# Up projections in split precision: one product over high and low activations, summed afterwards by VectorE

## The reference

```python
def sq_relu_mlp(h, w1, w2):                    # h 256 x 1024, w1 1024 x 4096, w2 4096 x 1024
    return jnp.square(jax.nn.relu(h @ w1)) @ w2
...
    u = rms_norm(x, ln2) @ w_up                # first block, the same with its residual
    return x + jnp.square(jax.nn.relu(u)) @ w_down
```

## Time and profile before

| | |
|---|---|
| median of 3 runs | 1900.62 us (1900.02 to 1901.37) |
| profiled execution, its own time | 1899.04 us |
| its span, first to last instruction | 1897.2 us |
| TensorE busy | 1821.4 us (96%), 11210 products |
| TensorE weight loads (overlap the products) | 1563.8 us, 11210 |
| VectorE busy | 1104.4 us (58%) |
| ScalarE busy | 916.0 us (48%) |
| mean granted TensorE clock | 0.984 of full speed |
| loads | 342.49 MB, mean 181 GB/s |

### The profile page before, as it was taken

The page is one execution under the profiler, slowest core; times in us unless marked ns, Lnnn a source line. Parts: engine busy times, 40 slices in busy tenths (PEclk is TensorE's granted clock), DMA queues, the critical chain, the costliest instruction groups (busy, mean ns, idle before and its releaser), DMA issues.

```text
span 1897.2 us, 26341 instructions
## 1 busy us (share of the span) xinstructions
PE 1821.4 (96%) x11210; PEld 1563.8 (82%) x11210; DVE 1104.4 (58%) x1247; ACT 916.0 (48%) x1211; POOL 38.4 (2%) x32
## 2 busy tenths in 40 slices
PE   7899999998999999999999999999999999989998
PEld 6768999787789989777899997778999787768997
DVE  4866555476665555466655555676555655766554
ACT  5455444354444445454545544645444545545442
POOL 0000000000000000000000000000000000000000
PEclk9999999899999999999999999999999999999999
DMA  7464656653656657653665555536665656344662
GB/s 243 134 214 145 197 180 196 202 167 130 214 178 185 192 189 233 207 193 129 211 194 183 189 184 184 193 111 200 188 189 188 213 176 216 109 163 149 185 190 77
DMA packets 228237, 342.49 MB, mean 181 GB/s; under 512 B 9909, under 2 KB 118809, under 8 KB 227993
## 3 DMA queue, kind: packets, MB, share of 16 engines
q1 hardware_dynamic: 226928, 339.45, 55.4%
q10 hardware_dynamic: 1192, 1.36, 0.2%
HBM read 339.74 MB, written 1.05 MB: 180 GB/s over the span
## 4 chain that ended last, share of the span: by engine, by line
PE 90%; DVE 5%; ACT 2%; issue 2%; POOL 1%; ACTq 0%; DVEq 0%; POOLq 0%
PE PS L1763 14%; PE PS L1765 14%; PE PS L1764 14%; PE PS L1805 9%; PE PS L1806 9%; PE PS L1807 9%; DVE LO L1114 1%; PE PS L2179 1%; PE PS L2149 1%; PE PS L2202 1%; PE PS L2131 1%; PE PS L2190 1%; PE PS L1838 1%; PE PS L2151 1%; PE PS L2150 1%
## 5 line engine op out<-in xcount | busy, mean ns | idle before, releaser
L1114 DVE TENSOR_TENSOR LO<-RAW,HI 128x2048 fp32r<-128x2048 f32 (+1 forms) x274 | 621.5, 2276 | 431.7 <-ACT HI L619 430.9
L619 ACT CAST HI<-RAW 128x2048 fp32r<-128x2048 f32 (+1 forms) x274 | 515.9, 1891 | 265.9 <-PE PS L1765 226.7
L1805 PE MATMUL PS<-AH,HI 128*128 128x256 f32 x1424 | 407.5, 286 | 2.2 <-DVE AL L1561 1.8
L1806 PE MATMUL PS<-AL,HI 128*128 128x256 f32 x1424 | 405.5, 285 | 0.0
L1807 PE MATMUL PS<-AH,LO 128*128 128x256 f32 x1424 | 405.3, 285 | 0.0
L1805 PEld LDWEIGHTS PS<-AH,HI 128*128 128x128 f32 x1424 | 276.3, 194 | 5.8 <-issue 5.2
L1806 PEld LDWEIGHTS PS<-AL,HI 128*128 128x128 f32 x1424 | 276.1, 194 | 1.1 <-issue 0.5
L1807 PEld LDWEIGHTS PS<-AH,LO 128*128 128x128 f32 x1424 | 275.9, 194 | 0.0
L1763 PE MATMUL PS<-HI,AH 128*128 128x512 f32 (+2 forms) x704 | 257.6, 366 | 0.0
L1765 PE MATMUL PS<-HI,AL 128*128 128x512 f32 (+2 forms) x704 | 252.0, 358 | 0.0
L1764 PE MATMUL PS<-LO,AH 128*128 128x512 f32 (+2 forms) x704 | 251.7, 358 | 0.0
(11 more groups left out here) (269 smaller groups left out, 1880.7 us busy)
## 6 DMA issues: line engine op xcount, KB each, us to landing
RAW<-in_w_ff SPq DMA_DIRECT2D x96, 1024.0 KB, 5.4
RAW<-in_w_in SPq DMA_DIRECT2D x80, 1024.0 KB, 5.2
RAW<-in_w_mod SPq DMA_DIRECT2D x48, 1024.0 KB, 5.1
RAW<-in_w_up SPq DMA_DIRECT2D x32, 1024.0 KB, 5.4
RAW<-in_w_down SPq DMA_DIRECT2D x32, 1024.0 KB, 5.0
RAW<-in_w_o SPq DMA_DIRECT2D x12, 1024.0 KB, 5.0
RAW<-in_w_out SPq DMA_DIRECT2D x8, 1024.0 KB, 6.2
RAW<-in_w_attn_out SPq DMA_DIRECT2D x6, 1024.0 KB, 5.7
```

Of the source, the lines that this page charges most:

```text
L619: return nc.scalar.copy(dst, src)
L1114: tt(LO[:, c % RAW_N, 0:n], RAW[:, c % RAW_N, 0:n], HI[:, NTH[c] % HL_N, 0:n].bitcast(F32), ALU.subtract).then_inc(s_lo, 1)
L1805: mm(o, wh, ah[:, j, :], start=j == 0, stop=False)
L1806: mm(o, wh, al[:, j, :], start=False, stop=False)
```

## The change

AH and AL become the two parts of one tile AHL, so that one moving operand of 2 × 256 columns holds both (two runs, 8 KB apart in each partition). For 14 of the 16 up chunks of each MLP (`wide`: all but j = 0 and 1 of i = 0), `features_wide` issues for each q and inner block one product wH·[aH | aL] of 512 columns into a whole bank, and one product wL·aH of 256 columns into that bank's first half. q = 0 and q = 1 have a bank each: 4 and 5 for odd j, 6 and 7 for even j. The result is the sum of a bank's two halves. ScalarE copies the first halves of both banks into U2 (`s_up`), VectorE adds the second halves (and frees the banks), and relu, square and remainder then read U2. The copy and the addition stand ahead of `ahead` in the code. TensorE has one wait more ahead of the transposes of i = 3, since their banks 6 and 7 are now also those of up chunks.

```diff
-        AH = sb("AH", [P, KT, S], F32R)
-        AL = sb("AL", [P, KT, S], F32R)
+        AHL = sb("AHL", [P, 2, KT, S], F32R)
+        AH, AL = AHL[:, 0, :, :], AHL[:, 1, :, :]
...
+        def wide(i, j):
+            return i > 0 or j > 1
+        def copies(q, i, j):
+            return 14 * q + 4 * i + j - 1
+        def wide_banks(j):
+            return 4 if j % 2 else 6
...
 # ScalarE, mlp
                     for j in range(8):
+                        if j < 4 and wide(i, j):
+                            b = wide_banks(j)
+                            act.wait_ge(s_used, c + 8 * i + j + late.n + 1 + HL_N)
+                            act.wait_ge(s_hl, 16 * q + 4 * i + j - 1)
+                            cast(U2[:, j % 2, :].rearrange("p (a n) -> p a n", a=2),
+                                 PS[:, b:b + 2, 0:256]).then_inc(s_up, 1)
                         ahead(c + 8 * i + j + late.n)
...
-                            act.wait_ge(s_used, c + 8 * i + j + late.n + 1 + HL_N)
-                            nc.scalar.activation(RL[:, j % 2, :], PS[:, 4 + (u + j) % 2, :], ACT.Relu).then_inc(s_rl, 1)
+                            if wide(i, j):
+                                act.wait_ge(s_ufree, u + 4 * i + j + 1 + 2)
+                                up = U2[:, j % 2, :]
+                            else:
+                                act.wait_ge(s_used, c + 8 * i + j + late.n + 1 + HL_N)
+                                up = PS[:, 4 + (u + j) % 2, :]
+                            nc.scalar.activation(RL[:, j % 2, :], up, ACT.Relu).then_inc(s_rl, 1)
...
 # VectorE, mlp
                     for j in range(8):
+                        if j < 4 and wide(i, j):
+                            b = wide_banks(j)
+                            dve.wait_ge(s_up, copies(q, i, j))
+                            up = U2[:, j % 2, :].rearrange("p (a n) -> p a n", a=2)
+                            tt(up, up, PS[:, b:b + 2, 256:512], ALU.add).then_inc(s_ufree, 1)
                         ahead(c + 8 * i + j + m.n)
...
-                            stt(U2[:, j % 2, :], PS[:, 4 + (u + j) % 2, :], 0.0, RL[:, j % 2, :], ALU.max,
-                                ALU.mult).then_inc(s_ufree, 1)
-                            dve.wait_ge(s_ufree, u + 4 * i + j + 1 + 2)
+                            if wide(i, j):
+                                link(stt(U2[:, j % 2, :], U2[:, j % 2, :], 0.0, RL[:, j % 2, :], ALU.max, ALU.mult))
+                            else:
+                                stt(U2[:, j % 2, :], PS[:, 4 + (u + j) % 2, :], 0.0, RL[:, j % 2, :], ALU.max,
+                                    ALU.mult).then_inc(s_ufree, 1)
+                                dve.wait_ge(s_ufree, u + 4 * i + j + 1 + 2)
...
 # TensorE
+            def features_wide(c, b):
+                arrived(c)
+                hi, lo = slot(c, KT, 256)
+                for q in range(2):
+                    for j in range(KT):
+                        wh, wl = hi[:, j, 128 * q:128 * q + 128], lo[:, j, 128 * q:128 * q + 128]
+                        mm(PS[:, b + q, :].rearrange("p (a n) -> p a n", a=2), wh, AHL[:, :, j, :],
+                           start=j == 0, stop=False)
+                        ins = mm(PS[:, b + q, 0:256], wl, AH[:, j, :], start=False, stop=j == KT - 1)
+                ins.then_inc(s_used, 1)
...
+                        if wide(i, j):
+                            features_wide(c + 8 * i + j + m.n, wide_banks(j))
...
+                        if e and i == 3 and j == 0:
+                            pe.wait_ge(s_ufree, u + 4 * i + 2 + 1 + 2)
```

More of the change, by code:

```diff
@@ L397, in build @@
         s_so = sem("output_gate")
+        s_up = sem("hidden_part_copied")
         s_rl = sem("hidden_relu")
@@ L1871, in mlp @@
                         first = i == 0 and j == 0
-                        features_out(c + 8 * i + j + (0 if first else m.n), 4 + (u + j) % 2, AH, AL,
-                                     ts if first else None, tiles if first else None, 1 + m.n if first else 1)
+                        if wide(i, j):
+                            features_wide(c + 8 * i + j + m.n, wide_banks(j))
+                        else:
+                            features_out(c + 8 * i + j + (0 if first else m.n), 4 + (u + j) % 2, AH, AL,
+                                         ts if first else None, tiles if first else None, 1 + m.n if first else 1)
                         if i == 0 and j == 1:
```

## The result

The changed kernel takes 1889.7 us in the median (1887.96 to 1892.68, 4 runs) against 1900.99 us before (1900.02 to 1901.66, 4 runs): 11.3 us less, ratio 0.9943 with a 95% interval from 0.9925 to 0.996. It is faster. The forecast was 1885.7 us, 14.9 us less, with a range of 1882 to 1896: the sign and the range hold, and three quarters of the forecast gain came. How much of that came from where the sum put it is another matter: in the profile the wide chunks saved 7.9 us, little more than half of the 14.9, and the rest came from elsewhere.

What follows compares the result with a forecast made beforehand. TensorE's product intervals were taken to bound the kernel: 0.213 us saved in each of 70 wide chunks makes 14.9 us, edits elsewhere cost nothing, so 1900.62 − 14.9 = 1885.7 us, range 1882 to 1896.

Steps and rivals of the forecast that it cites:

- What bounds the kernel: TensorE busy 96% of the span; in the MLPs nobody keeps it waiting, so only closer-spaced products win time.
- A product costs 13.3 ns beside its columns: At full clock each TensorE product has this fixed cost whatever its width; 16 fewer products save 0.213 us a wide chunk.
- I take the steady intervals: Alternating 512 and 256 products in wide chunks priced at 226.7 and 120.0 ns, 0.347 us a pair; 14.9 us less.
- the slow bound: In wide chunks a 512 always starts slowly, a 256 gains nothing: 0.355 us a pair, 5.6 us saved; partial gain, chance 0.09.
- The prediction's own sign: In an up chunk's timeline, starts alternate by about 0.227 and 0.120 us and the chunk takes 5.55 us.
- the 240 ns that it named as wrong: A 512 interval of 240 ns or more in the wide chunks would show the forecast wrong.
- The range: Forecast span of the whole kernel's time, likeliest case with partial gain: 1882 to 1896 us, leaving out 0.15.
- up to 3 us: Allowance in the kernel's time for stretches of lower clock that may fall elsewhere, giving about 1882 to 1888.5 us.
- Two runs as one moving operand: 512 columns from two 1 KB runs of 256 stream like a contiguous 512, 226.7 ns a product.
- the rival "no change": Each address run of a wide product's moving operand costs 13.3 ns, so 240 ns a product and 1900.6 us; chance 0.07.
- the slower operand: Wide products' two-run moving operand streams more slowly; beyond 240 ns a product the change loses, up to 2110 us; chance 0.04.
- Evacuation hidden: ScalarE's copies (41 us) and VectorE's additions (48 us) cost TensorE nothing; HIDL done at 6.4 us, cover left 4.4 us.

Runs made afterwards that it cites:

- the evacuation alone: The earlier kernel's 48 products of 256 columns with all of the changed kernel's new evacuation; 1899.95 us against 1899.44 for the kernel before, ratio 1.0.
- Grouped by chunks: Changed kernel with all sixteen 512-column products of a wide chunk first, then its sixteen of 256; 1887.23 us against 1900.14 for the kernel before.
- by banks: Changed kernel with, in each bank, eight products of 512 columns first, then eight of 256; 1886.93 us against 1899.44 for the kernel before.
- the contiguous run: Changed kernel with the 512 moving columns from two neighbouring AH blocks, hidden values differ; 1889.93 us against 1899.44 for the kernel before.
- the held-up relu: Changed kernel with ScalarE doing the relu of each turn's last up chunk twelve times more; 1945.92 us in a single run.
- by twos: Changed kernel with two products of 512, then two of 256, and so on in each bank; 1886.51 us against 1901.59 for the kernel before.
- alternating with a shifted block: Changed kernel with each 256 product taken from the inner block before that of the 512 ahead of it; 1888.63 us against 1900.92 before.
- by fours: Changed kernel with four products of 512, then four of 256, and so on in each bank; 1886.75 us in a single run.
- alternating with the other bank between: Changed kernel with widths nearly alternating but neighbouring products writing different banks; 1888.07 us in a single run.

## Why the prediction was right or wrong

- **What bounds the kernel: right.** TensorE's intervals set the time; with the evacuation alone nothing moved.
- **A product costs 13.3 ns beside its columns: right for runs of one width.** Grouped by chunks, sixteen products fewer a chunk saved 0.193 of the 0.213 us. The lower level of the earlier trace rows is read from its intervals, since the profile's granted clock is 1.00 there; where it is 0.5, at 372 us, products of 256 take 213 ns too.
- **"I take the steady intervals": this step failed.** Of the three values that the prediction had for a pair (0.345, 0.347, 0.355 us) the measured one is 0.353, next to the slow bound. The term was mis-sized: 14.9 us for 7.9 (7.5 by the copies). The first two rows at a change of width were read as cancelling: one 0.24 and one 0.11, each to 10 ns, can't settle a question of 7 ns. To the ns they are 233 and 113, and the mean over the changes in the trace before shows 233 and 236 ns for the first two products of 512 and 228, 233 and 231 for the next three, against 113 and 119 for the first two of 256 on the way back. That is 20 ns lost at each change to and fro between long runs, and the orders by banks and by chunks paid just this (0.040 and 0.020 us a chunk). For single products it wasn't to be had from the trace before: there the product of 512 takes 236 ns, as the slow bound has it, and the one of 256 takes 117, of the 10 ns that were hoped for only 3. The prediction's own sign, a chunk of 5.55 us, failed with 5.65, while the 240 ns that it named as wrong wasn't reached.
- **The range: right; the size, partly luck.** With the chunks' 7.9 us alone the time would be about 1892.7 us, still inside the range, and little more than half of the forecast gain. That three quarters came is owed to stretches of lower clock, which no term of the sum holds. The "up to 3 us" for them was about the size seen, 3.1 to 3.8.
- **Two runs as one moving operand: right at no cost**, and the rival "no change" (13.3 ns a second time) and the slower operand fall with the contiguous run's 5.653.
- **Evacuation hidden: right.** VectorE in the changed kernel (start us, duration), for the chunk whose copy begins at 583.43:

```profile
584.05 0.69 DVE L1244 TENSOR_TENSOR U<-U,PS 128x512 f32<-128x512 f32 x1 [0.23 <-ACT U L632]
585.86 2.29 DVE L1139 TENSOR_TENSOR LO<-RAW,HI 128x2048 fp32r<-128x2048 f32 x1 [1.11 <-ACT HI L632]
588.07 0.68 DVE L1263 SCALAR_TENSOR_TENSOR U<-U,RL 128x512 f32<-128x512 f32 x1
588.78 0.69 DVE L1269 TENSOR_TENSOR HIDL<-U,HIDH 128x512 fp32r<-128x512 f32 x1
```

  HIDL is done at 589.47, 6.2 us after the chunk's end (583.24), where 6.4 was placed. Busy time grew by 48 us of additions and 41 us of copies, as summed. What was not placed is the next stage's split in the last turn; it has the same engines and, as the held-up relu shows, its own cover to lose.

## What to carry to other kernels

Where TensorE is fed without waits, count its instructions as well as its columns: joining two products that share a stationary operand removes one fixed cost, and a second run of 1 KB in the moving operand was free here. Then measure the order: the same 32 products took from 5.567 to 5.653 us by order alone, least by sixteens of one width, nearly as little by twos, most one by one. And when less than 4 us in 1900 matter, compare durations of the same piece of work at the full clock in the traces, and medians of runs at the same granted clock, since where the lower clock falls moves a median by as much.

## What the runs showed of the hardware

- A float32r product with its own weight load takes 120.0 ns for 256 columns and 226.7 for 512 at the full clock, 213.3 and 426.7 at the lower one: 13.3 ns beside the columns at 2.4 GHz, nothing at 1.2 GHz. The Trainium skill ("TensorE: Matmul & The Clock Gate", "Wait — 56ns, not 53.3ns?") has about 2.5 ns for a warm product. Here it is 13.3, and the measurement decides.
- A pattern of 512 and 256 columns costs more than its parts, and below runs of four not in proportion to the changes. Excess over 5.547 us a chunk: alternating 0.106, alternating with a shifted block 0.093, by fours 0.066, by eights 0.040, alternating with the other bank between 0.040 to 0.051, by twos 0.026, by sixteens 0.020.
